# Expert items in a row on TensorE, turns on VectorE, a batched gather in split fp32r, and the scatter in one visit

## What is computed

```python
def moe_swiglu(x, router, wg, wu, wd):
    b, T, D = x.shape
    xt = x.reshape(b * T, D)
    logits = (xt @ router).astype(F32)
    top_v, top_i = lax.top_k(logits, TOP_K)
    wts = jax.nn.softmax(top_v, axis=-1)
    gates = jnp.sum(jax.nn.one_hot(top_i, N_EXPERTS, dtype=F32) * wts[..., None], axis=1)
    out = jnp.zeros_like(xt)
    for e in range(N_EXPERTS):
        ye = swiglu(xt, wg[e], wu[e], wd[e])
        out = out + ye * gates[:, e:e + 1].astype(xt.dtype)
    return out.reshape(b, T, D)
```

## Time and profile before

| | us |
|---|---|
| median of 3 runs | 1657.19 (1655.55 to 1657.95) |
| profiled execution, time | 1655.91 |
| profiled execution, span | 1654.1 |
| TensorE busy | 1596.0 |
| VectorE busy | 449.5 |
| ScalarE busy | 338.3 |
| first matmul of the expert items (gather of item 0) | at 613.90 |

### The profile page before, as it was taken

One profiled execution on the slowest core, in us unless ns is written; L12 is line 12 of the kernel. 1 busy time (PEld: TensorE's weight loads), 2 busy tenths in 40 slices (PEclk: granted clock), 3 DMA queues, 4 the chain that ended last, 5 costly groups with the idle time before them and its releaser, 6 DMA issues.

```text
span 1654.1 us, 45454 instructions
## 1 busy us (share of the span) xinstructions
PE 1596.0 (96%) x20372; PEld 1466.5 (89%) x20372; DVE 449.5 (27%) x824; ACT 338.3 (20%) x554; POOL 76.3 (5%) x88
## 2 busy tenths in 40 slices
PE   8998999999999999999989989989989989998996
PEld 7775799999598689999989989989989989998995
DVE  5487456654756521001001001001001001101101
ACT  4285344432465020001001001001001001001002
POOL 0070000000304200000000000000000000000000
PEclk9999999999899999999999999999999998999998
DMA  8331245565044169999979979979998997997970
GB/s 279 102 102 52 77 155 176 187 209 164 26 153 153 67 239 375 393 376 373 376 288 369 375 288 371 356 298 379 357 336 327 360 375 266 362 379 287 365 255 28
DMA packets 221407, 432.38 MB, mean 261 GB/s; under 512 B 9530, under 2 KB 76608, under 8 KB 220896
## 3 DMA queue, kind: packets, MB, share of 16 engines
q1 hardware_dynamic: 217960, 425.34, 71.8%
q10 hardware_dynamic: 3256, 4.06, 0.8%
HBM read 428.33 MB, written 1.05 MB: 260 GB/s over the span
## 4 chain that ended last, share of the span: by engine, by line
PE 92%; DVE 3%; issue 3%; ACT 1%; DMA 0%; ACTq 0%; DVEq 0%
PE ps L1609 89%; PE ps L1626 3%; DVE arena L1055 1%; ACT arena L772 1%; DVE arena L1197 0%; DVE arena L1165 0%; DVE arena L1171 0%; DMA ktab<-in_k_table_dram 0%; ACT arena L664 0%; DVE arena L1172 0%; DVE arena L1166 0%; DVE arena L1140 0%; DVE arena L1138 0%; DVE ring_lo L1263 0%; ACT ring_hi L851 0%
## 5 line engine op out<-in xcount | busy, mean ns | idle before, releaser
L1609 PE MATMUL ps<-raw,xg 128*32 128x384 f32 (+1 forms) x9216 | 532.2, 380 | 0.0
L1609 PEld LDWEIGHTS ps<-raw,xg 128*32 128x32 f32 x9216 | 509.8, 110 | 9.0 <-issue 7.9
L1609 PE MATMUL ps<-raw,ehT 128*32 128x384 f32 (+1 forms) x4608 | 268.0, 383 | 5.8 <-issue 5.1
L1609 PEld LDWEIGHTS ps<-raw,ehT 128*32 128x32 f32 x4608 | 255.6, 110 | 10.4 <-issue 7.9
L1500 DVE TENSOR_TENSOR eh<-esg,ps 128x384 f32<-128x384 f32 x56 | 31.0, 554 | 734.5 <-PE ps L1609 734.5
L1609 PE MATMUL ps<-xn_hi,ring_hi 128*128 128x272 f32 x544 | 159.2, 293 | 0.9 <-DVE crd L1375 0.8
L1609 PE MATMUL ps<-xn,ring 128*128 128x272 f32 (+1 forms) x640 | 157.4, 406 | 0.9 <-DVE xn L1055 0.8
L1609 PE MATMUL ps<-xn_hi,ring_lo 128*128 128x272 f32 x544 | 157.9, 290 | 0.0
L1609 PE MATMUL ps<-xn_lo,ring_hi 128*128 128x272 f32 x544 | 157.0, 289 | 0.0
L1609 PEld LDWEIGHTS ps<-xn,ring 128*128 128x128 f32 x640 | 125.6, 198 | 30.0 <-issue 5.2
L984 ACT ACTIVATE ehT<-ps 128x384 f32<-128x384 f32 x56 | 27.5, 492 | 605.4 <-PE ps L1626 588.9
(11 more groups left out here) (289 smaller groups left out, 1298.0 us busy)
## 6 DMA issues: line engine op xcount, KB each, us to landing
raw<-in_moe_w_gate_dram SPq DMA_DIRECT2D x96, 1024.0 KB, 6.7
raw<-in_moe_w_up_dram SPq DMA_DIRECT2D x96, 1024.0 KB, 7.3
raw<-in_moe_w_down_dram SPq DMA_DIRECT2D x96, 1024.0 KB, 6.5
raw_ring<-in_moe_w_down_dram SPq DMA_DIRECT2D x16, 1024.0 KB, 8.5
raw_ring<-in_moe_w_gate_dram SPq DMA_DIRECT2D x16, 1024.0 KB, 7.3
raw_ring<-in_moe_w_up_dram SPq DMA_DIRECT2D x16, 1024.0 KB, 6.9
ring<-in_w_in_ab_dram SPq DMA_DIRECT2D x12, 1024.0 KB, 6.4
ring<-in_hy_w_in_dram SPq DMA_DIRECT2D x12, 1024.0 KB, 5.1
```

Of the source, the lines that this page charges most:

```text
L1609: return nc.tensor.matmul(o, l, r, start=start, stop=stop)
```

## The change

- TensorE's items 1 to 7 are written out one after another; only the later items keep a loop. ScalarE and VectorE keep loops, split at item 4.
- The turn of the hidden tile goes from TensorE to VectorE: 16 transposes of 32x32 blocks (three blocks each) per stage, straight from `eh` to `ehT`, which gets two halves. ScalarE's copy from bank 2 falls away.
- The gather is done for four experts at once, before item 0 and before item 4. `SEL` holds four experts (384 columns) and is fp32r; the tokens are split in `xtk_hi` and `xtk_lo`, both fp32r, so that there are four matmuls of 128x384 for each of eight tiles, on four banks in turn (`GATHER`). ScalarE copies the even tiles, VectorE the odd ones. `xtk_lo` is made by four new VectorE operations before item 0 (`turned_rows_low`).
- The scatter's four tiles come in one visit after j = 1 of stage 2, on four banks. VectorE's four additions come after the product of stage 2.
- `turn_table` reads the gate column from the table itself for items 0 to 7, and waits for the additions of the item before.

The core of the diff:

```diff
-        xtk = xn[:].rearrange("p k t -> p (k t)")[:, 0:2 * D].rearrange("p (t d) -> p t d", t=2)
+        xtk_hi, xtk_lo = overlay("xtk_hi", 0, 2, D), overlay("xtk_lo", KT * T, 2, D)
-        ehT = sb("ehT", [P, GROUPS, P])
-        SEL = sb("SEL", [P, 2, CAP])
+        SEL = sb("SEL", [P, 2, BATCH, CAP], F32R)
+        ehT = sb("ehT", [P, 2, GROUPS, P])
+        GATHER = (6, 7, 2, 3)
@@ ScalarE
-            def turned_hidden(i, p, S):
-                act.wait_ge(sem("turned"), S + 1)
-                if p is not None:
-                    act.wait_ge(sem("unit_used"), consumed(i, p))
-                nc.scalar.activation(ehT[:].rearrange("p a b -> p (a b)"), bank[2][:, 0:MAIN], ACT.Copy).then_inc(sem("ehT_ready"), 1)
+            def gathered(before, width):
+                for d in range(0, KT, 2):
+                    act.wait_ge(sem("gather_ready"), before + d + 1)
+                    nc.scalar.activation(xg[:, 0:width, d, :], bank[GATHER[d % 4]][:, 0:width * CAP].rearrange("p (e c) -> p e c", e=width),
+                                         ACT.Copy).then_inc(sem("xg_even"), 1)
@@ VectorE
+            def select_batch(b):
+                for tt in range(2):
+                    mine = place[:, NI * tt + BATCH * b:NI * tt + BATCH * b + BATCH].rearrange("p (e a) -> p e a", a=1).to_broadcast([P, BATCH, CAP])
+                    each = iota.rearrange("p (a c) -> p a c", a=1).to_broadcast([P, BATCH, CAP])
+                    V.tensor_tensor(SEL[:, tt, :, :], each, mine, ALU.is_equal).then_inc(sem("sel_ready"), 1)
+            def turned_rows_low(half):
+                group = ("xk", "xm")[half]
+                for tt in range(2):
+                    c = slice(512 * half, 512 * half + 512)
+                    dve.wait_ge(sem("xtk_high"), 2 * half + tt + 1)
+                    t = ready(dve, group, tt)
+                    v(V.scalar_tensor_tensor(out=xtk_lo[:, tt, c], in0=t[:, :], scalar=rs[:, tt:tt + 1], in1=xtk_hi[:, tt, c].bitcast(F32),
+                                             op0=ALU.mult, op1=ALU.subtract), used(group))
-            select(0)
+            select_batch(0)
+            turned_rows_low(0)
+            turned_rows_low(1)
+            def turn_hidden(i, s, first=False):
+                dve.wait_ge(sem("h_ready"), STAGES * i + s + 1)
+                if s >= 2:
+                    dve.wait_ge(sem("unit_used"), consumed(i, down_at(s - 1, 1)))
+                elif not first:
+                    dve.wait_ge(sem("unit_used"), consumed(i, (down_at(0, 1), 1)[s]))
+                for q in range(4):
+                    for g in range(4):
+                        src = eh[GROUP * g:GROUP * g + GROUP, :].rearrange("p (b c) -> p b c", b=GROUPS)[:, :, GROUP * q:GROUP * q + GROUP]
+                        V.transpose(ehT[GROUP * q:GROUP * q + GROUP, s % 2, :, GROUP * g:GROUP * g + GROUP], src).then_inc(sem("ehT_ready"), 1)
@@ VectorE, item
-                    if s == 2 and not first:
-                        add_result(i, 0)
-                        add_result(i, 1)
                     hidden(i, s)
                     if s == 2 and not first:
-                        add_result(i, 2)
-                        add_result(i, 3)
+                        for c in range(4):
+                            add_result(i, c)
+                    turn_hidden(i, s, first)
@@ TensorE
-            def gather(i):
-                pe.wait_ge(sem("sel_ready"), 4 * i + 2)
+            def gather(before, width, first=False, j=None):
                 for d in range(KT):
...
+                    if first and d < 4:
+                        pe.wait_ge(*((used("xk"), 2), (used("pos"), 1), (sem("row_rstd"), 1), (used("xm"), 2))[d])
+                    if d >= 4:
+                        copied = (before // 2 if isinstance(before, int) else KT // 2 * j + KT) + d // 2 - 1
+                        pe.wait_ge(sem("xg_odd" if d % 2 else "xg_even"), copied)
+                    o = bank[GATHER[d % 4]][:, 0:CAP * width]
                     for tt in range(2):
-                        o = bank[6 + d // 4][:, CAP * (d % 4):CAP * (d % 4) + CAP]
-                        last = mm(o, xtk[:, tt, P * d:P * d + P], SEL[:, tt, :], tt == 0, tt == 1)
+                        mm(o, xtk_hi[:, tt, P * d:P * d + P], SEL[:, tt, 0:width, :].rearrange("p e c -> p (e c)"), tt == 0, False)
+                        last = mm(o, xtk_lo[:, tt, P * d:P * d + P], SEL[:, tt, 0:width, :].rearrange("p e c -> p (e c)"), False, tt == 1)
@@ TensorE, item
-                gather(i)
+                if isinstance(i, int) and i % BATCH == 0:
+                    b = i // BATCH
+                    pe.wait_ge(sem("sel_ready"), 2 * b + 2)
+                    if b:
+                        pe.wait_ge(sem("comb_used"), 4 * i - 4)
+                        pe.wait_ge(sem("selt_ready"), 2 * i)
+                    gather(KT * b, BATCH, first)
...
                     gate_up(i, s, 0)
-                    if s or not first:
-                        turn_hidden(S + (s - 1), first and s == 1)
...
                     if s == 2 and not first:
-                        add_result(i, 0)
-                        add_result(i, 1)
+                        add_result(i)
...
             item(0, True)
-            with pe.Fori(1, NE) as i:
+            for i in range(1, NE):
                 item(i)
```

More of the change, by code:

```diff
@@ L322, in trunk @@
         sb("held", [P, 12 * 2048])
[L323 to L326, removed]
-        ehT = sb("ehT", [P, GROUPS, P])
-        SEL = sb("SEL", [P, 2, CAP])
+        unit = [raw[:, r, :] for r in range(12)] + [raw_ring[:, r, SLOT - 2048:SLOT] for r in range(2)]
+        xg = sb("xg", [P, BATCH, KT, CAP])
+        SEL = sb("SEL", [P, 2, BATCH, CAP], F32R)
+        rt = sb("rt", [P, 640])
         SELT = sb("SELT", [P, SEQ], F32R)
@@ L1014, in item @@
                         scatter_table(i)
-                    if s or not first:
-                        turned_hidden(i, None if first and s == 1 else 1 if s == 0 else down_at(s - 1, 1), S + (s - 1))
                     silu(i, s)
+            gathered(0, BATCH)
             item(0, True)
-            with act.Fori(1, NE) as i:
+            with act.Fori(1, BATCH) as i:
+                item(i)
+            gathered(KT, BATCH)
+            with act.Fori(BATCH, NE) as i:
                 item(i)
@@ L1544, in later_table, with item @@
                     v(V.tensor_reduce(gate3[:, tt, NE:ITEMS], prod3, AX.X, ALU.add))
[L1546 to L1550, removed]
+            def item(i, first=False, then=None):
                 for s in range(STAGES):
@@ L1572, in _ @@
                 with dve.Fori(0, more) as j:
-                    item(j + NE)
+                    gathered(KT * j + 2 * KT, 1)
+                    item(j + NE, then="later")
             result(more + NE, 3)
@@ L2078, in gate_up, with down @@
                     kk = 4 * (j % 2) + k
-                    rows = [xg[:, kk, GROUP * g:GROUP * g + GROUP] for g in range(GROUPS)]
+                    rows = [xg[:, e, kk, GROUP * g:GROUP * g + GROUP] for g in range(GROUPS)]
                     last = columns(bank[j // 2], rows, w[:, k, :], kk == 0, kk == KT - 1)
                 last.then_inc(sem("unit_used"), 1)
-            def turn_hidden(S, first=False):
-                pe.wait_ge(sem("h_ready"), S + 1)
-                if not first:
-                    pe.wait_ge(sem("ehT_ready"), S)
-                for c in range(GROUPS):
-                    last = turn(bank[2][:, P * c:P * c + P], eh[:, P * c:P * c + P])
-                last.then_inc(sem("turned"), 1)
-            def down(i, at, S, begin=False, end=False, units=(0, 1)):
-                pe.wait_ge(sem("ehT_ready"), S + 1)
-                for j in units:
+            def down(i, at, S, s, begin=False, end=False):
+                pe.wait_ge(sem("ehT_ready"), 16 * (S + s) + 16)
+                for j in range(2):
                     p = at + j
@@ L2099, in down @@
                         b = 2 * j + k
-                        rows = [ehT[:, b, GROUP * g:GROUP * g + GROUP] if b < GROUPS else ehT[:, g, CAP:P] for g in range(GROUPS)]
+                        rows = [ehT[:, s % 2, b, GROUP * g:GROUP * g + GROUP] if b < GROUPS else ehT[:, s % 2, g, CAP:P] for g in range(GROUPS)]
                         for half in range(2):
@@ L2118, in gather, with add_result @@
-            def gather(i):
-                pe.wait_ge(sem("sel_ready"), 4 * i + 2)
-                for d in range(KT):
-                    if isinstance(i, int) and d == 4:
-                        pe.wait_ge(used("pos"), 1)
-                        pe.wait_ge(used("xm"), 2)
+            def add_result(i):
+                pe.wait_ge(sem("ye_split"), 2 * i)
+                pe.wait_ge(sem("selt_ready"), 2 * i)
+                if not isinstance(i, int) or i > 1:
+                    pe.wait_ge(sem("comb_used"), 4 * i - 4)
+                for c in range(4):
+                    for d in range(2):
```

(6 more changed lines are left out.)

119 lines of the change are left out of this document (62 added, 57 removed).

## The result

The changed kernel takes 1557.97 us (median of 4 runs, 1552.91 to 1561.29), against 1656.52 for the kernel before in the same comparison. The ratio is 0.9402, 95% interval 0.9373 to 0.9431.

The account below looks back on a forecast made before the run. TensorE, busy for 96% of the span, was taken to bound the kernel. Terms -26.9 - 73.4 + 7.5 + 5.5 = -87.3 us against 1655.91 gave 1568.6, stated as 1569, range 1560 to 1588.

Parts of the forecast that it names:

- turns off TensorE: Expert stages: moving the hidden tile's turns to VectorE saves 56 visits of 0.48 us, 26.9 us.
- passages, items 1 to 7: Between expert items: gathers, gaps at TensorE's loop jump back and slow clock go, 73.4 us less.
- second gather: Before item 4: new batched gather of 32 matmuls, with 1.9 us of wait for VectorE, adds 7.5 us (4.0 to 12).
- first gather: Before item 0: first expert matmul 4.5 us later, plus 1 us for a falling clock: 5.5 us (3 to 10).
- scatter: Stage 2 of an item: same 16 matmuls in one visit, VectorE's additions moved behind the product; 0 us.
- exit: End of the item loop: the 33.9 us to the end stay, as the jump past later items remains; 0 us.
- their cover: VectorE's transposes hide behind expert matmuls; tightest at stage 0 to 1, 6.2 us with copies against 10.6 us; cost 0.
- the rival of late weights: Expert items: at 365 GB/s sustained DMA, weights come late beyond the cushion, 1591 us; chance 0.08.
- the margin: Expert items: DMA at 391 to 393 GB/s keeps up with the 385 GB/s needed by 2%.
- the bounds of terms 3 and 4: Second gather 4.0 to 12 us and first gather 3 to 10 us, setting the forecast's own range.
- the forecast's own range: Whole kernel: 1561 to 1578 us, from the bounds of the two gathers; chance 0.77.

Follow-up runs that it names:

- experiment 2: Changed kernel with three unused fp32 identity transposes per visit put back on TensorE behind each stage's first gate unit; 1595.88 us, ratio 0.9629.
- experiment 1: Kernel before the change with only TensorE's items 1 to 7 written out instead of looped; 1605.57 us, ratio 0.9682.
- experiment 9: Changed kernel with the scatter's four tiles in two visits again, on the same four banks; 1562.00 us, ratio 0.9409.
- experiment 7: Changed kernel with VectorE's four copies of the second gather ahead of the 16 transposes of item 3's last stage; 1553.02 us, ratio 0.9365.
- experiment 3: Changed kernel with one unused fp32 identity transpose per visit put back on TensorE; 1582.27 us, ratio 0.9536.
- experiment 4: Changed kernel with every VectorE block transpose done twice, the extra one into a spare tile; 1558.68 us, ratio 0.9394.
- experiment 6: Changed kernel without TensorE's block for later items, so no count read and no jump over it; 1550.05 us, ratio 0.9342.
- experiment 5: Changed kernel with every VectorE block transpose done three times, two into spare tiles; 1575.41 us, ratio 0.9501.

## Why the prediction was wrong, step by step

| term | forecast, us | measured, us | from |
|---|---|---|---|
| turns off TensorE | -26.9 | -33.9 | 0.62 each, 55 visits up to the exit (experiment 2) |
| passages, items 1 to 7 | -73.4 | -74 | six periods 47.6 less (experiment 1), seven gathers of 3.77 |
| second gather | +7.5 | +10.2 | items 3 and 4: 9.8 and 0.4 over 113.04 |
| first gather | +5.5 | +4.7 | 15.23 against 10.58 from the logits to the first expert matmul |
| scatter | 0 | -2.3 | 0.33 per item (experiment 9) |
| exit | 0 | -3.4 | 30.38 to 27.00 (25.97 in four other traces of this exit) |
| sum | -87.3 | -98.7 | -99.3 between the traces |

**1, the turns.** The step that failed is "a visit takes 0.48 us", read from the start of the transposes to the start of the next expert matmul. The mechanism was right and the term too small by 0.13 us, which 56 visits made 7 us, more than half of the miss. The number that would have been right stood in the earlier trace rows too, in part: two stages start 750.30 - 733.97 = 16.33 us apart, and of that I called 15.86 us "expert matmuls". But the 15.86 already hold 0.14 us that only a stage with a visit has. A stage without one is 15.72 us in the changed kernel:

```profile
838.82 5.16 PE L1642 MATMUL ps<-raw,ehT 128*32 128x384 f32 x90
...
854.54 5.16 PE L1642 MATMUL ps<-raw,ehT 128*32 128x384 f32 x90
```

The price of 0.27 us per transpose was exact, and their cover held; a sequence of 16 takes 4.8 us with the spacing, not 4.3. The rule in the Trainium skill ("VectorE: DVE Perf Modes", Rules for kernel authors) that a 128x128 transpose belongs on TensorE would have cost 34 us here, where TensorE is the bound and VectorE isn't. The estimate of 160 ns by the cycle formula on that page of the Trainium skill was low against the 270 ns measured.

**2, the passages.** Right to within 1 us, and experiment 1 shows the cause.

**3, the second gather.** Right in what waits for what (VectorE's transposes ahead of its copies, 2.43 us of wait against 1.9 forecast). What I left out is the clock: in the trace of the changed kernel it fell behind this wait and nearly doubled the distance of the last matmuls (0.17 to 0.32 us), and item 4 lost 0.6 us by it (113.40 against 112.75 in experiment 7). I had put such a fall at the first gather, where it didn't happen.

**4, the first gather.** The order of events came as written; all of the 1 us for the clock was too much.

**5, the scatter.** I looked for a wait and found none, and so put the term at 0. I didn't ask what a second visit costs by itself: 0.3 us, seven times.

**6, the exit.** "Stays" was wrong: the second pause, a part of the slow clock behind it and the last turn with its copy and wait of 0.7 us are gone. Experiment 1 has 3.0 of the 3.4 us, with the turn still in place. That the pause goes is not something the change aimed at, and two relatives of the changed kernel have it (experiments 2 and 3): this part of the gain is luck as far as the runs show.

**DMA.** It moved 375 GB/s in item 0 and 387 to 392 in items 1 to 3, and TensorE never waited for weights. An item of 113.04 us needs 390 GB/s for its 44.0 MB, so the rival of late weights was wrong, but with a margin thinner than forecast: the items came out shorter than the 114.5 us that the margin was worked out for.

**What stays open.** Some 0.6 us of the 99.3 aren't in the table. Why the clock falls behind the 2.43 us wait in some executions and not in others isn't shown, nor why the untouched front part varies, nor what in a jump takes TensorE's time. The batched gather has no experiment of its own; its terms are read from the traces.

**The range.** All of its terms were bounded, except that the turns, the scatter and the exit had no bound on the side of a larger gain. Each of the three came out on that side. There is also a slip: the bounds of terms 3 and 4 give 1569 - 3.5 - 2.5 = 1563 as the lower end of the forecast's own range, and not 1561.

## What to carry to other kernels

Price a piece of work that interrupts a dense stream of matmuls by the period of the stream with and without it, or by a dummy visit, not by the distance of two starts: here a fifth of the price lay outside. When TensorE is the bound, every jump back of its loop is an item of the sum, and so is each separate visit, even one that moves nothing new. Work moved to an idle engine is free up to its deadline, and TensorE waits for what is over it: find the tightest deadline first, here 10.5 us of one stage, of which the transposes and copies need 6.7.

## What the runs showed of the hardware

- A jump back of TensorE's loop costs 4.3 to 5.5 us of standing still, and then a stretch at 1.2 GHz; 7.9 us per passage here (experiment 1). At the jump forward at the exit TensorE stands still for 3.2 to 3.7 us over all traces that have it, and in three of them a second time (1.55, 2.02 and 2.41 us).
- Leaving a stream of four side-by-side fp32 matmuls and coming back costs 0.29 us; a 128x128 fp32 transpose in between adds 0.11 us (experiments 2 and 3). A second visit for the scatter costs 0.33 us (experiment 9).
- A 32x96 fp32 block transpose on VectorE takes 0.27 us, 0.30 apart. In the pairs of experiment 4 the second takes 0.23 us, and a pair 0.46.
- fp32r matmuls of 384 columns start 0.17 us apart at 2.4 GHz and 0.32 us apart at 1.2 GHz (1071.72 to 1071.89, 1073.06 to 1073.38 above).
- The profile named ehT for a gap that was a jump, and "issue" for a wait that VectorE's transposes made (experiments 6 and 5).
